# Loading one parameter tile first, moving the end of the step-size chain into round one, taking the last norm into the MLP's last round, and 128 bytes of padding in SBUF

## The chip, the cores and the metric

The kernel runs on one core of a Trainium2 chip. The metric is the device time of one execution in microseconds (us); lower is better. The kernel before took 2057.4 us in the median of three runs (2056.34 to 2058.93).

## The reference

The reference is two transformer-like blocks on 512 tokens of width 1024, all in float32. Cut to what matters here:

```python
# first block, part one: SSD mixer
u = rmsnorm(x, ssd_norm)
z, xbc, dt = split(u @ ssd_w_in)
xbc = silu(dwconv(xbc, conv_w, conv_b))          # 5 taps
dt = softplus(dt + dt_bias)                      # 512 tokens x 64
la = dt * -exp(a_log);  cum = cumsum(la) per chunk of 128 tokens, forwards and backwards
y = ssd_scan(...) both ways + x * d_skip; y = rmsnorm(y * silu(z), gnorm)
h = x + y @ ssd_w_out
# then: GLA mixer, mixing block (conv, latent attention, gates), cross attention
h = h + square(relu(rms_norm(h, norm_mlp_g) @ w_mlp1)) @ w_mlp2
return rms_norm(h, final_norm_g)                 # 512 x 1024
```

## The kernel before

**Layout and matmuls.** Activations lie transposed: `c.h`, `c.uh`, `c.ul` are eight tiles (`KT`) of 128 features by 512 tokens. A float32 product is three matmuls (`mm3`, L57 to L67): operands are split into a rounded part (`hi`, float32r) and the rest (`lo`), and lo times hi, hi times lo and hi times hi are added in PSUM. The weights come in units of 128x1024 elements. `load_unit` (SP, L112) loads one into one of `RAW` = 2 slots and waits until the unit two before it was split; `split_hi` (ScalarE, L123) rounds it into one of `WS` = 3 slots and waits for the matmuls of the unit three before; `split_lo` (VectorE, L133) makes the rest. `stream_products` (TensorE) runs a unit's 24 matmuls of 128x512 into one of `SB` = 3 PSUM banks ("stream") and waits for the bank to be free. The five other banks are `q[0]` to `q[4]`. Each engine works through its own instructions in the order of the code and waits on semaphores.

**Opening (in `ssd_stage`, first block).** SP issues the loads of x (four, L461), of two weight units, of 128 rows of `ssd_conv_w` (tile 0 of the parameter rows), of two vectors, of the other parameter rows (22 small loads for parameters in all, four tiles `c.ptiles`) and then of weight units. TensorE turns the four parameter tiles (L510), VectorE copies each to `par` (L616). ScalarE sums the squares of x (L570) and takes the rough reciprocal root (L574, L576). Only then does VectorE refine it (L170 to L176), and x is scaled by VectorE (L620) and ScalarE (L579), two row tiles each. TensorE turns the scaled x (L518), ScalarE and VectorE make `uh` (L584) and `ul` (L625) with the gain `ssd_norm`, and the product for dt (unit `first`) runs between them. Then the units `first+1` and `first+2` are streamed, and x is turned into `c.h` (L525, L599). Meanwhile VectorE works on the softplus of dt, its logarithmic decays and their sums (L631 to L661, "the step-size chain"). TensorE then turns dt, la and cum (12 small transposes, L555) once VectorE has done with `cum_l` (L666), VectorE copies them (L670 to L672), TensorE sums the columns (L559), and ScalarE and VectorE make `et`, `wc`, `lah`, `lal` (L604 to L607, L675 to L688). Last, `first+3` is streamed.

**Rounds.** A second block runs ten rounds of eight slots `(i, k)`, written out in the same order for each engine. Round 0 has the units `(0,2)`, `(0,3)`, `(0,5)`, `(0,6)`, that are `first+1` to `first+4`: x, x, B and C of group 0. The convolution of a unit stands in the slot after it: ScalarE does the middle tap (L959), VectorE the four others (L1081), which also frees the bank. At slot `(0,7)` ScalarE takes the silu (L1027, L1029), at `(1,0)` TensorE streams a unit, waits for the silu and turns the results (L913). POOL makes the decay steps (L810) from `lah`, `lal`. Blocks and stages are parted by a barrier of all engines.

**MLP and end.** `mlp_stage` streams 64 units, in turn eight that read `uh`/`ul` (first product, closed by L2747) and eight that read `ah`/`al` (second product, added to `h` at L2761). In the last eight, ScalarE squares `h` (L191) and POOL adds up the squares (L206). `norm_stage` ("last") then sums over the features with a matmul with ones (L317, or q<-h_sum_of_squares), refines the reciprocal root over 128x512 and scales all of `h` (L362). `finish_stage` turns `h` back (32 transposes, L2783), copies it to `out_rows` (L2791, L2797) and stores four row tiles (L2804).

**Where the tiles lie.** In the compiled program a tile follows the one before it in the order of the code, sizes rounded up to 32 bytes. Byte offsets in a partition, and the remainder by 256:

```
u_hi 32896 (128)         weights_hi 73856 (128)   weights_lo 86144 (128)
u_lo 49280 (128)         h_squares 102080 (192)   params 108224 (192)
ssd_y_hi 198400 (0)      merge_hi 179968 (0)      mix_cq_hi 151296 (0)
x_q_hi 184064 (0)        mlp_a_hi 118528 (0)      mlp_a_lo 134912 (0)
gla_q_hi 137152 (192)    gla_y_hi 210880 (192)
```

Parts of a tile that a matmul reads begin at multiples of 512 bytes in it, so each has the remainder of its tile.

## Time and profile before

| | |
|---|---|
| median of 3 runs | 2057.4 us (2056.34 to 2058.93) |
| the profiled execution | 2057.16 us |
| its span, first to last instruction | 2055.4 us |
| TensorE matmul busy | 1829.1 us (89%) |
| VectorE, ScalarE, GpSimd busy | 1264.9, 783.8, 418.3 us |
| mean granted TensorE clock | 0.946 |
| read from HBM, mean rate | 135.70 MB, 67 GB/s |

The span is one execution as the hardware profiler recorded it. The profiled execution took 1.8 us more than its span. PE is TensorE, PEld its weight loads, DVE VectorE, ACT ScalarE, POOL GpSimd, SPq the queue of SyncE that issues the loads. "<-" inside a name reads "written from".

### The profile page before, as it was taken

The numbers are of one execution on the slowest core, as the hardware profiler recorded it, in microseconds if no ns is written. First come the engines' busy times: TensorE is split into PE (matmuls) and PEld (weight loads), VectorE is DVE, ScalarE is ACT, GpSimd is POOL, SyncE is SP. The second block draws the span as 40 slices with busy tenths as digits, with TensorE's granted clock in tenths as the row PEclk, the third lists the DMA queues.
The fourth block names the chain that finished last, engine by engine and source line by source line (L and its number), as shares of the span: only waits on it lengthen the run. The fifth ranks groups of instructions, "written<-read, shape, count | busy, mean of one in ns | idle before, by whom it ended". The sixth has DMA issues, their size and how long they took to land. (4 is left out here: it accounts for less than half of the span.)

```text
span 2055.4 us, 21726 instructions
## 1 busy us (share of the span) xinstructions
PE 1829.1 (89%) x8186; PEld 1460.3 (71%) x8186; DVE 1264.9 (62%) x1665; ACT 783.8 (38%) x1165; POOL 418.3 (20%) x369
## 2 busy tenths in 40 slices
PE   5789999999977989999978997787899799999996
PEld 4667777777754868787856776565678778888884
DVE  4668877887766555656546779765465553434343
ACT  4432443344324352535234423344344442323232
POOL 0244644464352000000006023400021020000001
PEclk9989999999988999999988999898899999999998
DMA  3212222222101212222212322110223133333331
GB/s 92 72 42 62 62 62 62 62 62 62 62 23 53 72 41 77 68 82 62 80 44 57 92 68 65 41 25 27 92 83 102 32 91 103 93 93 102 93 93 51
DMA packets 252197, 139.19 MB, mean 68 GB/s; under 512 B 25973, under 2 KB 246558, under 8 KB 252094
## 3 DMA queue, kind: packets, MB, share of 16 engines
q1 hardware_dynamic: 252093, 137.82, 23.4%
q8 instruction: 65, 1.06, 0.2%
q14 instruction: 39, 0.31, 0.0%
HBM read 135.70 MB, written 2.10 MB: 67 GB/s over the span
## 5 line engine op out<-in xcount | busy, mean ns | idle before, releaser
L65 PE MATMUL stream<-u_lo,weights_hi 128*128 128x512 f32 (+2 forms) x1312 | 535.3, 408 | 46.8 <-DVE weights_lo L133 19.3
L133 DVE TENSOR_TENSOR weights_lo<-weights_raw,weights_hi 128x1024 fp32r<-128x1024 f32 (+4 forms) x266 | 341.0, 1282 | 308.1 <-ACT weights_hi L123 307.8
L67 PE MATMUL stream<-u_hi,weights_hi 128*128 128x512 f32 (+2 forms) x1312 | 521.1, 397 | 0.0
L66 PE MATMUL stream<-u_hi,weights_lo 128*128 128x512 f32 (+2 forms) x1312 | 521.1, 397 | 0.0
L123 ACT ACTIVATE weights_hi<-weights_raw 128x1024 fp32r<-128x1024 f32 (+4 forms) x266 | 268.1, 1010 | 470.4 <-PE stream L67 430.1
L65 PEld LDWEIGHTS stream<-u_lo,weights_hi 128*128 128x128 f32 (+2 forms) x1312 | 252.1, 192 | 123.6 <-issue 34.5
L67 PEld LDWEIGHTS stream<-u_hi,weights_hi 128*128 128x128 f32 (+2 forms) x1312 | 250.9, 191 | 56.6 <-issue 0.9
L66 PEld LDWEIGHTS stream<-u_hi,weights_lo 128*128 128x128 f32 (+2 forms) x1312 | 251.8, 192 | 54.9 <-issue 3.4
L203 POOL COPY h_sum_of_squares<-h_squares 128x512 f32<-128x512 f32 x5 | 3.2, 650 | 856.9 <-ACT h_squares L191 856.9
L67 PE MATMUL stream<-mlp_a_hi,weights_hi 128*128 128x512 f32 x256 | 101.1, 395 | 0.0
L65 PE MATMUL stream<-mlp_a_lo,weights_hi 128*128 128x512 f32 x256 | 101.1, 395 | 0.0
L66 PE MATMUL stream<-mlp_a_hi,weights_lo 128*128 128x512 f32 x256 | 101.1, 395 | 0.0
L1986 DVE SCALAR_TENSOR_TENSOR mix_conv<-mix_z,params,mix_conv 128x512 f32<-128x512 f32 x79 | 82.1, 1040 | 2.3
L769 POOL TENSOR_TENSOR ssd_y<-ssd_y,ssd_state_parts 128x384 f32<-128x384 f32 x32 | 33.1, 1035 | 190.7 <-DVE ssd_state_parts L1067 188.4
L1081 DVE SCALAR_TENSOR_TENSOR ssd_bc<-stream,params,ssd_bc 128x510 f32<-128x510 f32 (+1 forms) x64 | 48.0, 749 | 33.3 <-ACT ssd_bc L959 31.6
L206 POOL TENSOR_TENSOR h_sum_of_squares<-h_sum_of_squares,h_squares 128x512 f32<-128x512 f32 x35 | 50.7, 1447 | 73.0 <-ACT h_squares L191 71.1
L2747 DVE SCALAR_TENSOR_TENSOR mlp_relu<-stream,h_squares 128x512 f32<-128x512 f32 x32 | 22.1, 691 | 69.2 <-PE stream L67 68.9
L1961 POOL TENSOR_TENSOR mix_conv<-mix_conv,gates_tap_products 128x512 f32<-128x512 f32 x30 | 46.4, 1546 | 76.1 <-ACT gates_tap_products L1953 74.0
L65 PE MATMUL stream<-ssd_y_lo,weights_hi 128*128 128x512 f32 x128 | 53.7, 419 | 7.8 <-DVE ssd_y_lo L1169 5.2
L66 PEld LDWEIGHTS stream<-mlp_a_hi,weights_lo 128*128 128x128 f32 x256 | 48.1, 188 | 11.7
L65 PEld LDWEIGHTS stream<-mlp_a_lo,weights_hi 128*128 128x128 f32 x256 | 48.1, 188 | 11.7
L67 PEld LDWEIGHTS stream<-mlp_a_hi,weights_hi 128*128 128x128 f32 x256 | 48.0, 188 | 11.6
(494 smaller groups left out, 3368.0 us busy)
## 6 DMA issues: line engine op xcount, KB each, us to landing
weights_raw<-in_w_mlp_dram SPq DMA_DIRECT2D x64, 512.0 KB, 3.9
weights_raw<-in_ssd_w_in_dram SPq DMA_DIRECT2D x48, 512.0 KB, 3.9
weights_raw<-in_gla_w_in_dram SPq DMA_DIRECT2D x40, 512.0 KB, 3.7
weights_raw<-in_w_in_dram SPq DMA_DIRECT2D x29, 512.0 KB, 3.7
weights_raw<-in_ssd_w_out_dram SPq DMA_DIRECT2D x16, 512.0 KB, 3.5
weights_raw<-in_gla_w_out_dram SPq DMA_DIRECT2D x16, 512.0 KB, 3.3
weights_raw<-in_w_out_dram SPq DMA_DIRECT2D x8, 512.0 KB, 4.0
weights_raw<-in_w_xkv_dram SPq DMA_DIRECT2D x8, 512.0 KB, 4.2
```

Source lines behind the costliest of these rows:

```text
L65: pe.matmul(out, lh, rl, start=first, stop=False, skip_group_check=skip)
L66: pe.matmul(out, ll, rh, start=False, stop=False, skip_group_check=skip)
L67: return pe.matmul(out, lh, rh, start=False, stop=last, skip_group_check=skip)
L123: act.activation(w_view(c, n)[0], raw_view(c, n), ACT.Copy).then_inc(c.w_rounded, 1)
L133: dve.tensor_tensor(lo, raw_view(c, n), hi.bitcast(F32), ALU.subtract).then_inc(c.w_split, 1)
L203: pool.tensor_copy(acc[:, :], c.sq[:, n % 2, :]).then_inc(c.square_added, 1)
L206: pool.tensor_tensor(acc[:, :], acc[:, :], c.sq[:, n % 2, :], ALU.add).then_inc(c.square_added, 1)
L769: pool.tensor_tensor(y[:, p, a], y[:, p, a], parts[:, d * (T - P):(d + 1) * (T - P)], ALU.add).then_inc(s_fin, 1)
L1081: ins = dve.scalar_tensor_tensor(out=dst[:, a:b], in0=src[:, a + o:b + o], scalar=tap(tp, ct), in1=dst[:, a:b], op0=ALU.mult, op1=ALU.add)
L1961: pool.tensor_tensor(acc[:, LAST, :], acc[:, LAST, :], prod[:, e % 2, :], ALU.add)\
L1986: dve.scalar_tensor_tensor(out=acc[:, m, :], in0=src, scalar=par[:, w:w + 1], in1=acc[:, m, :], op0=ALU.mult, op1=ALU.add)\
L2747: dve.scalar_tensor_tensor(out=r_[:, m % 2, :], in0=bank(c, t)[:, :], scalar=0.0, in1=c.rstd, op0=ALU.max, op1=ALU.mult).then_inc(c.bank_f ...
```

## The change

1. `ssd_norm` becomes the first vector of the parameters, so tile 0 holds it and 120 rows of `ssd_conv_w`. Tile 0 is loaded before the first two weight units, the other tiles after them. VectorE waits for tile 0 only before it refines the root of x; three row tiles of x are scaled by VectorE and one by ScalarE. The other parameter tiles are turned into `q[4]` after the product for dt and copied by one VectorE instruction after the step-size chain's sums.
2. The opening's block ends with unit `first+2`. What followed `cum` (the 12 transposes, the copies, the column sums, `et`, `wc`, `lah`, `lal`) stands in slots `(0,4)` to `(0,7)`, unit `first+3` in `(0,5)`. The tiles dt, la, cum and their columns live as long as the stage (9,216 bytes a partition). ScalarE's table load at the start of the second block goes. In the opening's block units up to `first+4` are loaded and split, one fewer.
3. The last norm is made inside `mlp_stage`: `h` is scaled by the gain, turned by TensorE between the last units, and scaled by token afterwards, when the tokens lie on partitions. The stages "last" and "out" go.
4. `stage_offset`, 128 bytes a partition, is allocated ahead of `params` and all stage tiles; `gla_rstd` grows from 64 to 128 bytes. Stage tiles' offsets grow by 128, those of GLA after `rstd` by 192, all to a remainder of 128 by 256.

```diff
@@ opening, SP
+                    load_params(0)
                     for n in range(first, first + 2):
                         load_unit(c, sp, n)
+                    ... (the two vectors)
+                    for i in range(1, NP):
+                        load_params(i)
...
-                    for n in range(first + 2, first + 6):
+                    for n in range(first + 2, first + 5):
@@ opening, TensorE
                     pe.wait_ge(s_const, 1)
-                    for i in range(NP):
-                        turn_params(i)
+                    turn_params(0)
...
                     last.then_inc(c.tile_done, 1)
+                    pe.wait_ge(s_par, 1)
+                    for i in range(1, NP):
+                        turn_params(i)
...
                     stream_products(c, pe, first + 2, ...)
-                    (12 transposes, column sums, stream_products of first + 3)
@@ opening, VectorE
-                    for i in range(NP):
-                        dve.wait_ge(s_pt, i + 1)
-                        n = c.prows[i]
-                        dve.tensor_copy(c.par[:, i * P:i * P + n], c.q[i][:, 0:n]).then_inc(s_par, 1)
+                    dve.wait_ge(s_pt, 1)
+                    dve.tensor_copy(par[:, 0:P], c.q[4][:, 0:P]).then_inc(s_par, 1)
                     dve.wait_ge(s_rx, 2)
                     refine_rstd(dve, s_fine, 0, rx[:, :], tx[:, :], ssq[:, :], D)
-                    for t in (0, 1):
+                    for t in (0, 1, 2):
...
+                    dve.wait_ge(s_pt, NP)
+                    n = P * (NP - 2) + c.prows[-1]
+                    dve.tensor_copy(par[:, P:P + n], c.q[4][:, 0:n]).then_inc(s_par, 1)
@@ rounds, VectorE, after the convolution of the slot before
+                    if (i, k) == (0, 5):
+                        dve.wait_ge(s_a, 4)
+                        (cum_l)
+                        dve.wait_ge(s_t, 1)
+                        (copies dtc, lac, cumc)
+                    if (i, k) == (0, 6):
+                        dve.wait_ge(s_t, 2)
+                        (cumc = q[0] - cumc)
+                    if (i, k) == (0, 7):
+                        dve.wait_ge(s_a, 7)
+                        (wc, lah, lal)
@@ rounds, ScalarE
-                act.preload_act_table_set(LN_EXP)
...
+                    if (i, k) == (0, 5):
+                        (cum_h)
...
+                    if (i, k) == (0, 7):
+                        act.wait_ge(s_v, 18)
+                        (exp of cumc, exp of q[0], round lac)
@@ rounds, TensorE: 12 transposes at (0,4); at (0,5) after the unit:
+                        pe.wait_ge(s_v, 16)
+                        pe.matmul(q[0][:, 0:NT * 64], c.ones[:, :], flat(lac), start=True, stop=True).then_inc(s_t, 1)
@@ rounds, POOL, before the first decay steps
+                            pool.wait_ge(s_v, 21)
@@ mlp_stage, TensorE
+                def to_rows(m):
+                    pe.wait_ge(s_hg, m + 1)
+                    if m == NT:
+                        pe.wait_ge(s_half, NT)
+                    for t in range(NT):
+                        last = pe.transpose(c.q[t][:, m % NT * P:(m % NT + 1) * P], hg[:, m, t * P:(t + 1) * P],
+                                            c.ident[:, :])
+                    last.then_inc(s_tp, 1)
+                def token_sums(src, first):
+                    for t in range(NT):
+                        last = pe.matmul(c.q[4][:, t:t + 1], src[:, t * P:(t + 1) * P], c.ones[:, 0:1], ...)
...
                 for k in range(N):
+                    if k - LAST >= 2:
+                        to_rows(k - LAST - 2)
                     (unit n0 + k)
+                to_rows(KT - 2)
+                pe.wait_ge(c.square_added, squares)
+                token_sums(c.sumsq, True)
+                pe.wait_ge(c.square_ready, squares + 1)
+                token_sums(c.sq[:, squares % 2, :], False).then_inc(s_tok, 1)
+                to_rows(KT - 1)
@@ mlp_stage, ScalarE, behind the square of unit k - 1
+                    if k == LAST + 5:
+                        act.preload_act_table_set(LN_EXP)
+                        act.wait_ge(s_tp, NT)
+                        for t in range(NT):
+                            act.activation(rows[:, t, 0:T], c.q[t][:, :], ACT.Copy).then_inc(s_half, 1)
+                (rough root of q[4][:, 0:NT], 128x4: Ln, Exp)
+                act.wait_ge(s_fine, 4)
+                act.wait_ge(s_tp, KT)
+                for t in range(NT):
+                    act.activation(rows[:, t, T:D], c.q[t][:, :], ACT.Copy, scale=rt[:, t:t + 1]).then_inc(s_right, 1)
@@ mlp_stage, GpSimd
-                add_squares(c, pool)
+                add_squares(c, pool, tiles=KT - 1)
@@ mlp_stage, VectorE
+                        if k > LAST:
+                            dve.wait_ge(*free_value(c, t))
+                            dve.tensor_scalar(hg[:, m, :], c.h[:, m, :], gain(m), None, ALU.mult).then_inc(s_hg, 1)
...
+                dve.wait_ge(s_root, 2)
+                refine_rstd(dve, s_fine, 0, rt[:, :], tmp[:, :], c.q[4][:, 0:NT], D)
                 for t in range(NT):
+                    dve.wait_ge(s_half, t + 1)
+                    dve.tensor_scalar(rows[:, t, 0:T], rows[:, t, 0:T], rt[:, t:t + 1], None, ALU.mult)\
+                       .then_inc(s_left, 1)
@@ mlp_stage, SP
+                for t in range(NT):
+                    sp.wait_ge(s_left, t + 1)
+                    sp.wait_ge(s_right, t + 1)
+                    sp.dma_start(o[:, t, :], rows[:, t, :]).then_inc(c.stored, 16)
+                sp.wait_ge(c.stored, 16 * NT)
@@ build and gla_stage
+        sb("stage_offset", [P, 32])
-        ssq, rstd = sb("square_sums", [P, NT]), sb("rstd", [P, 16])[:, 0:NT]
+        ssq, rstd = sb("square_sums", [P, NT]), sb("rstd", [P, 32])[:, 0:NT]
-        norm_stage(nc, c, "last", ...)
-        finish_stage(nc, c, out)
```

## Rows read from the trace of the kernel before

**Rows 1.** The timeline, 10 to 26 us: start, length, engine, line, what, count.

```profile
10.71 0.21 ACT L576 ACTIVATE dt_x_rstd<-dt_x_rstd 128x4 f32<-128x4 f32 x1
...
17.70 0.36 SPq L476 DMA_DIRECT2D dt_skips<-in_ssd_d_dram  x1
...
19.11 0.20 DVE L616 COPY params<-q 128x41 f32<-128x41 f32 x1 [1.44 <-PE q L510]
...
20.01 2.19 ACT L579 ACTIVATE dt_x_normed<-dt_x_rows,dt_x_rstd 128x1024 f32<-128x1024 f32 x2 [9.09 <-DVE dt_x_rstd L176]
20.01 1.42 DVE L620 TENSOR_SCALAR dt_x_normed<-dt_x_rows,dt_x_rstd 128x1024 f32<-128x1024 f32 x2
...
22.25 3.67 PE L518 MATMUL q<-ident,dt_x_normed 128*128 128x128 f32 x16 [3.18 <-ACT dt_x_normed L579]
```

**Rows 2.** The timeline, 34 to 56 us, TensorE and VectorE.

```profile
34.19 1.91 PE L525 MATMUL q<-ident,dt_x_rows 128*128 128x128 f32 x16
...
51.01 1.22 DVE L661 TENSOR_TENSOR_SCAN dt_cum<-dt_restart,dt_la 32x512 f32<-32x512 f32 x1
...
54.13 0.46 PE L555 MATMUL q<-ident,dt_dt 64*128 64x64 f32 x4 [2.91 <-DVE ssd_cum_lo L666]
...
55.93 1.22 PE L559 MATMUL q<-dt_la_cols,ones 128*128 128x256 f32 x2 [0.85 <-DVE dt_la_cols L671]
```

**Rows 3.** The timeline, 55 to 84 us, by engine: TensorE, ScalarE and VectorE in round 0.

```profile
55.79 0.41 DVE L672 COPY dt_cum_cols<-q 128x256 f32<-128x256 f32 x1
...
59.68 2.35 DVE L133 TENSOR_TENSOR weights_lo<-weights_raw,weights_hi 128x1024 fp32r<-128x1024 f32 x2
...
63.77 1.28 ACT L942 ACT_TABLE_LOAD   x1 [3.23 <-PEq L457]
...
65.88 6.11 DVE L1081 SCALAR_TENSOR_TENSOR ssd_x<-stream,params,ssd_x 128x510 f32<-128x510 f32 x8 [3.85 <-ACT ssd_x L959]
...
69.13 0.76 PE L65 MATMUL stream<-u_lo,weights_hi 128*128 128x512 f32 x1 [5.64 <-DVE ssd_x L1081]
...
76.50 0.78 ACT L959 ACTIVATE ssd_bc<-stream,params 128x512 f32<-128x512 f32 x1 [6.88 <-PE stream L67]
...
77.31 3.10 DVE L1081 SCALAR_TENSOR_TENSOR ssd_bc<-stream,params,ssd_bc 128x510 f32<-128x510 f32 x4 [1.18 <-ACT ssd_bc L959]
...
83.86 1.09 PE L913 MATMUL q<-ident,ssd_x 128*128 128x128 f32 x8 [1.96 <-ACT ssd_bc L1029]
```

**Rows 4.** The timeline, 2012 to 2051 us: last units, last norm, output.

```profile
2015.28 0.63 ACT L191 ACTIVATE h_squares<-h 128x512 f32<-128x512 f32 x1 [1.89 <-DVE h L2761]
...
2017.87 0.69 DVE L2761 TENSOR_TENSOR h<-h,stream 128x512 f32<-128x512 f32 x1 [2.62 <-PE stream L67]
...
2029.07 0.69 DVE L2761 TENSOR_TENSOR h<-h,stream 128x512 f32<-128x512 f32 x1 [4.92 <-PE stream L67]
...
2050.66 0.69 DVE L2797 COPY out_rows<-q 128x512 f32<-128x512 f32 x1 [0.18 <-PE q L2783]
```

**Rows 5.** The timeline of VectorE: two closings of each kind of MLP unit.

```profile
1885.07 0.69 DVE L2747 SCALAR_TENSOR_TENSOR mlp_relu<-stream,h_squares 128x512 f32<-128x512 f32 x1 [2.41 <-PE stream L67]
...
1890.51 0.69 DVE L2747 SCALAR_TENSOR_TENSOR mlp_relu<-stream,h_squares 128x512 f32<-128x512 f32 x1 [2.41 <-PE stream L67]
...
1903.84 0.68 DVE L2761 TENSOR_TENSOR h<-h,stream 128x512 f32<-128x512 f32 x1
...
1909.43 0.68 DVE L2761 TENSOR_TENSOR h<-h,stream 128x512 f32<-128x512 f32 x1
```

**Rows 6.** The page: DMA issues, KB each, median us from issue to landing.

```profile
weights_raw<-in_ssd_w_in_dram SPq DMA_DIRECT2D x48, 512.0 KB, 3.9
```

**Rows 7.** Busy time by engine, granted clock, DMA share and rate in one stretch.

```profile
2052.00:2053.00 1.00, 0.00 (x0) 0.00 (x0) 0.00 (x0) 0.00 (x0) 0.00 (x0) 1.00 1.02 418
```

**Rows 8.** The timeline of TensorE, first and last matmul of the unbroken run over `gla_y`.

```profile
1072.66 0.41 PE L65 MATMUL stream<-gla_y_lo,weights_hi 128*128 128x512 f32 x1
...
1092.37 0.39 PE L67 MATMUL stream<-gla_y_hi,weights_hi 128*128 128x512 f32 x1
```

More of the change, by code:

```diff
@@ L191, in square_tile, with add_squares @@
         act.activation(c.sq[:, n % 2, :], c.h[:, m, :], ACT.Square).then_inc(c.square_ready, 1)
-def add_squares(c, pool, accs=None):
+def add_squares(c, pool, accs=None, tiles=KT):
     accs = accs or [c.sumsq]
-    for m in range(KT):
+    for m in range(tiles):
         for acc in accs:
@@ L462, in _, with load_params @@
                           .then_inc(s_xl[t], 16)
-                    for n in range(first, first + 2):
-                        load_unit(c, sp, n)
-                    for i, tile in enumerate(c.ptiles):
-                        for r0, view in tile:
+                    def load_params(i):
+                        for r0, view in c.ptiles[i]:
                             dst = prow[r0:r0 + view.shape[0], i, :]
@@ L550, in _ @@
                     stream_products(c, pe, first + 2, lambda j: c.uh[:, j, :], lambda j: c.ul[:, j, :])
-                    pe.wait_ge(s_v, 14)
-                    pe.wait_ge(s_h, KT)
-                    for j, src in enumerate((dt, la, cum)):
-                        for t in range(NT):
-                            last = pe.transpose(c.q[1 + j][:, t * 64:(t + 1) * 64], src[:, t * P:(t + 1) * P],
-                                                c.ident[0:64, 0:64])
-                    last.then_inc(s_t, 1)
-                    pe.wait_ge(s_v, 16)
-                    pe.matmul(c.q[0][:, 0:NT * 64], c.ones[:, :], lac[:, :, :].rearrange("p t h -> p (t h)"),
-                              start=True, stop=True).then_inc(s_t, 1)
-                    stream_products(c, pe, first + 3, lambda j: c.uh[:, j, :], lambda j: c.ul[:, j, :])
                 @block.scalar
@@ L1038, in _ @@
             def _(dve):
-                for n in range(first, first + 2):
-                    split_lo(c, dve, n)
                 taps = [0]
@@ L2674, in cross_stage, with mlp_stage @@
         cross_out_stage(nc, c, A, qh, ql, gain)
-def mlp_stage(nc, c, A):
+def mlp_stage(nc, c, A, out, gain):
     CH = FF // D
@@ L2691, in mlp_stage @@
         tile = lambda k: c.tiles_before[n0 + k]
+        hg = sb("h_scaled", [P, KT, T])
+        rows = sb("out_rows", [P, NT, D])
+        rt, tmp = sb("token_rstd", [P, NT]), sb("token_newton", [P, NT])
+        o = out[0].rearrange("(t p) d -> p t d", p=P)
+        s_hg, s_tp, s_half, s_tok, s_root, s_fine, s_left, s_right = (sem(n) for n in (
+            "h_scaled", "transposed", "first_half", "token_sums", "token_rstd_s", "token_refined",
+            "left_rows", "right_rows"))
+        squares = c.added + KT - 1
+        LAST = N - KT
         with nc.Block() as block:
```

149 lines of the change are left out of this document (60 added, 89 removed).

## The prediction

> **What bounds the kernel now.** First the page: TensorE is busy for 89% of the span, and in the MLP its 64 units follow each other without a gap. So there are two ways to a shorter time: fewer stretches in which TensorE stands, and a closer sequence of matmuls where it doesn't. I then read the timeline at both ends. At the start the first transposes of x begin at 22.25 us, because the last parameter copy on VectorE began only at 19.11 and the refined root stands behind it; the rough root was there at 10.92 [rows 1]. In round 0 TensorE stands twice more: 2.91 us for the step-size chain, and 5.64 us for a bank that the taps free [rows 2, 3]. At the end, TensorE does its last streamed matmul just before 2029.07, and 26.3 us follow in which the norm and the output run one after the other [rows 4]. Last, I compared the closings of MLP units: one that reads `u` takes 5.44 us, one that reads `mlp_a` 5.59, with the same weights, shapes and engines [rows 5].
>
> All sums are in the profiled execution's time: span 2055.4, and 2057.16 with what lies around it (1.8 us), which is within 0.3 us of the median of 2057.4.
>
> **Part 1, the opening.** The rough root stands at 10.92. Parameter tile 0 is now issued right behind x, and x was in before the root was taken, so I take it as landed and copied by 10.9, when the root needs it. From the start of the last copy to the start of the scaling took 0.90 us before (19.11 to 20.01), so scaling starts at 11.8. VectorE scaled two row tiles in 1.42, so three take 2.13: 13.95. ScalarE does its one tile (1.10) and the rounding inside that. TensorE starts at about 14.0 instead of 22.25: **8.3 us earlier** [rows 1]. What could be late next: the queue of SP. It has the same loads in another order and ends them at about 18.1 as before [rows 1]; only then does it issue unit `first+2`. A unit lands 3.9 us after its issue [rows 6], so at 22; it is due after the transposes of x that began at 34.19 and unit `first+1`, so after 41 minus 8.3. That leaves 10 us of cover [rows 2]. The 22 small loads are no longer in anyone's way: their transposes (three, under 0.5 us) stand after the dt product, and it is VectorE's chain, for which TensorE waits 2.91 us later, that sets the end of this block [rows 2]. Bounds: 6 us if tile 0 lands 2 us after the root, 8.5 if all goes at once.
>
> **Part 2, the chain into round 0.** I keep the old times here; all are 8.3 lower in fact. The scans end at 52.23 [rows 2]. Then VectorE copies the other parameters (0.47, from 0.41 for 256 columns), does the three small copies (0.5) and splits two units (2.35) [rows 3]: 55.6. The barrier took 0.28 before (the last matmul ended 5.64 before 69.13, at 63.49; the first instruction behind it is at 63.77), so round 0 starts at 55.9 instead of 63.77. The table load (1.28) is gone from it: the first taps start 0.8 after the start, at 56.7, and their 8 take 6.11: 62.8. Now the moved work: `cum_l` and three copies, each started before the one ahead has ended, 1.75 (0.41 is the row for a copy, 0.7 for twice its width), 64.6, and the split of `first+5` 1.2, 65.8. TensorE meanwhile does 12 transposes (0.95) and unit `first+3`. It starts after 5 us of rest, so at the lower level of its clock (1.2 GHz), as the unit at 69.13 did, with 7.3 us for 24 matmuls: 64.3. Its middle tap (0.78) is done when VectorE comes. Taps 3.1: 68.9. The column sums (0.66) go ahead of `first+4` on TensorE, 65.0; that unit 5.5, 70.5; middle tap, 71.3; taps, 74.4. Before, these taps ended at 80.41 [rows 3]. So another **6.0 us**. `wc`, `lah`, `lal` (1.1 us on VectorE, then POOL's four steps) are late next: POOL can start at 75.6 and needs 4.2, and the first decay sums come some 8 us after the transposes at 77.9. ScalarE's three small ones (1.2) stand before the silu but are done at 72.5. Queued behind TensorE's wait for `lac` is only `first+4`; `lac` is copied at 64.2, before the unit ends. Bounds: 4 (the taps of B wait, each moved copy counts fully) to 7.
>
> **Part 3, the end.** Added inside the loop: six groups of four transposes. Sixteen took 1.91, so 0.12 each and 2.9 us, on a TensorE that never waits there. `to_rows(4)` waits for `s_half`: the square of the unit ended at 2015.91, then comes the table load 1.28 and four copies of about 0.5 (squares of that size take 0.63), so 2019.2; TensorE gets there 0.5 after 2017.8, at 2018.3 [rows 2, 4]. So 0.9 more. Scaling by the gain on VectorE (8 of under 0.7) is hidden: between two closings 5.6 us apart VectorE has one split (1.2) and the addition (0.68) to do [rows 5].
> After the last closing (2029.07, call it T): `h` 0.69, square 0.63, so T+1.4; the first half of the token sums and `to_rows(6)` run under that. The second half is eight passes of one column. No row shows one: below by the 0.12 of a transpose, above by the 0.6 of a pass over 256 columns [rows 2]; nearest is the transpose, a load of 128 columns and little else, so 1.0. T+2.4. Ln and Exp on 128x4 0.8 with their starts, refinement 0.8, four scaled copies 2.0 (VectorE's four lie beside them). The first row tile can go at T+4.7, the last at T+6.1. The store moves 2.1 MB; in the stretch where it is alone it went at 418 GB/s [rows 7], so 5.0 us in all, 1.25 a tile. Before, the end came 4.05 after the last row tile was copied (2051.35 to 2055.4) [rows 4]. So not before T+6.1+4.05, T+10.2, and at most three tiles' transfers behind the first tile's 4.05, T+12.5. Four issued within 1.4 us are bound by the transfer, so near the upper end: T+11.9. Before, it was T+26.3. **14.4 less 3.8 is 10.6 us.** Bounds: 8 (token sums at the upper bound, copies one by one) to 12.5.
>
> **Part 4, the padding.** Offsets of `u` and of the weights leave 128 by 256. `mlp_a`, `merge`, `x_q`, `mix_cq` and `ssd_y` leave 0, GLA's leave 192. Two MLP units differ by 0.16 us over 24 matmuls, so 226.7 against 233 ns from start to start [rows 5]. The unbroken run over `gla_y`, 86 steps, gives 19.71/86 = 229.2 [rows 8], in between, at a third remainder. That the level goes with the remainder and not with the stage is shown by the MLP, where both kinds alternate. If a remainder of 128 gives 226.7 to all: MLP 32 units, 5.1 us; 384 `ssd_y`, 192 `merge`, 96 `x_q`, 120 latent matmuls at 0.0067 are 5.3, of which I count 3.3, since TensorE partly waits for VectorE in those stages; 384 `gla_y` at 0.0025 1.0. Sum **9.4 us**. What stays open is whether 256 is the period: by 512 the moved tiles leave 384, `u` 128. Bounds: none at all to 12. I take the full value, as five families of tiles fit it.
> The Trainium skill ("TensorE: Matmul & The Clock Gate", section "Wait — 56ns, not 53.3ns?") gives a warm matmul of 512 columns 215.7 ns from start to start, whatever its operands' addresses; by it this part would be worth nothing. The trace doesn't agree: it has 226.7 and 233.
>
> **Sum.** 8.3 + 6.0 + 10.6 + 9.4 = 34.3. 2055.4 - 34.3 = 2021.1, and with 1.8 around the span **2022.9 us**.
>
> **Rivals.** (a) The remainder isn't the cause, and the padding does nothing. For it: every slower family also lies above 110,000 bytes, `u` below 66,000; against it: `gla_y` lies highest of all and is the middle one. 2032.3. Chance 0.13. "SBUF — State Buffer", section "Who interferes with whom", of the Trainium skill would side with it: PE never waits on anyone. (b) The transposes break the stream of the last round: the wait for `s_half` or another one lets the clock fall, and nine matmuls run at 0.43 instead of 0.23, as after 69.13 [rows 3], and each of the six groups costs 0.3 more when TensorE changes between kinds. +1.8 and +1.8: 2026.5. For it, the clock did fall after 5.6 us of standing; against, this wait is 1 us. Chance 0.08. (c) The loads are late: unit `first` and `first+1` now stand behind tile 0, and ScalarE's rounding of a unit that has not landed holds up all that stands behind it, `uh` too. If the dt product then starts 8.3 us later than said, where it did before, 2031.2. Against it, two small loads are all that goes ahead of them. Chance 0.04. (d) Slower: the new remainder by 512 is a worse one. Some 1900 matmuls move, and the other parts give 24.9 us, so this decides from 13 ns more for each, twice the difference between the levels seen. The price at three times that difference, 20 ns, is 38 us: 2070. Chance 0.02. That the change does nothing in parts 1 and 3 I can exclude: 26 us of serial work are taken out.
>
> **How the numbers follow.** The forecast has 0.73, with an own range of 2019 to 2027. To hold 8 in 10 with (b) and most of (a), the range is 2018.5 to 2032.8. 0.2% (4.1 us) is about what a measurement of this kernel can tell from no change. Faster 0.97; same 0.01; slower 0.02.
>
> **What would show it.** The transposes of scaled x start at 14.0; those after the silu 14.3 earlier than 83.86, at 69.6. MLP units over `mlp_a` close every 5.44 us instead of 5.59; if it is 5.59, (a) holds. In the last round one gap of 0.9 us ahead of the fifth group of transposes. From the last closing to the end of the span 12 us. The forecast is wrong above all if the remainder does nothing, or if the moved tiles fall on a third level.

## The result and the profile after

The changed kernel takes 2024.44 us in the median of four runs (2023.38 to 2032.84); the kernel before, run beside it, 2058.16 (2056.34 to 2064.12). The ratio is 0.9841, with a 95% interval of 0.9818 to 0.9863. The profiled execution took 2024.04, its span is 2022.3. The forecast was 2022.9 (2018.5 to 2032.8) and "faster" at 0.97.

The page of the changed kernel: the span, and TensorE's busy time.

```profile
span 2022.3 us, 21708 instructions
...
PE 1813.3 (90%) x8200; PEld 1456.5 (72%) x8200; DVE 1259.3 (62%) x1664; ACT 782.1 (39%) x1167; POOL 414.5 (20%) x368
```

TensorE does almost the same matmuls and is busy 15.8 us less than the 1829.1 of before. Of that, 3.4 lie ahead of the transposes after the silu and 4.8 behind the last matmul over `mlp_a`; the other 7.6 lie between, where the same work runs closer together. The rest of the 33.1 us of span is standing time: 21.5 us less at the two ends, some 4 us more between them.

**The opening.** The timeline of the changed kernel, all engines, from the rough root to the first transposes (start, length, engine, line, what, count, what it waited for).

```profile
10.26 0.44 PE L510 MATMUL q<-ident,dt_param_rows 128*128 128x128 f32 x1 [10.26 <-DMA dt_param_rows<-in_ssd_conv_w_dram]
...
10.74 0.29 DVE L595 COPY params<-q 128x128 f32<-128x128 f32 x1 [10.74 <-PE q L510]
...
11.16 0.21 ACT L565 ACTIVATE dt_x_rstd<-dt_x_rstd 128x4 f32<-128x4 f32 x1
...
12.20 2.08 DVE L599 TENSOR_SCALAR dt_x_normed<-dt_x_rows,dt_x_rstd 128x1024 f32<-128x1024 f32 x3
...
14.33 3.29 PE L516 MATMUL q<-ident,dt_x_normed 128*128 128x128 f32 x16 [3.63 <-DVE dt_x_normed L599]
```

The one parameter copy is over when the rough root comes at 11.37 (11.16 and 0.21), so nothing stands ahead of the refinement any more. The transposes start at 14.33 instead of 22.25 [rows 1]: 7.9 earlier.

**Round 0.** The timeline of VectorE, ScalarE and TensorE from the last parameter copy to the transposes after the silu.

```profile
42.82 0.47 DVE L644 COPY params<-q 128x297 f32<-128x297 f32 x1
...
46.52 1.45 ACT L937 ACTIVATE ssd_x<-stream,params 128x512 f32<-128x512 f32 x2 [5.61 <-PEq L454]
...
47.34 6.11 DVE L1062 SCALAR_TENSOR_TENSOR ssd_x<-stream,params,ssd_x 128x510 f32<-128x510 f32 x8 [1.10 <-ACT ssd_x L937]
...
56.09 3.09 DVE L1062 SCALAR_TENSOR_TENSOR ssd_bc<-stream,params,ssd_bc 128x510 f32<-128x510 f32 x4
...
62.00 3.10 DVE L1062 SCALAR_TENSOR_TENSOR ssd_bc<-stream,params,ssd_bc 128x510 f32<-128x510 f32 x4 [1.36 <-ACT ssd_bc L937]
...
68.56 1.09 PE L892 MATMUL q<-ident,ssd_x 128*128 128x128 f32 x8 [1.97 <-ACT ssd_bc L1012]
```

From the end of the scans (42.8) to the round's first instruction it is 3.7 us, where the forecast had 52.23 to 55.9. The last taps end at 65.1, 18.6 after the round's start, where the forecast had 74.4 - 55.9 = 18.5. The transposes start at 68.56 instead of 83.86 [rows 3], 15.3 earlier (forecast 14.3).

**The last round.** VectorE's closings of two pairs of units over `mlp_a` and over `u`, then ScalarE, VectorE and TensorE at the fifth group of transposes.

```profile
1904.87 0.68 DVE L2814 TENSOR_TENSOR h<-h,stream 128x512 f32<-128x512 f32 x1
1910.31 0.68 DVE L2814 TENSOR_TENSOR h<-h,stream 128x512 f32<-128x512 f32 x1
...
1929.78 0.69 DVE L2800 SCALAR_TENSOR_TENSOR mlp_relu<-stream,h_squares 128x512 f32<-128x512 f32 x1 [2.41 <-PE stream L67]
1935.22 0.69 DVE L2800 SCALAR_TENSOR_TENSOR mlp_relu<-stream,h_squares 128x512 f32<-128x512 f32 x1 [2.41 <-PE stream L67]
...
1994.09 0.63 ACT L191 ACTIVATE h_squares<-h 128x512 f32<-128x512 f32 x1 [1.89 <-DVE h L2814]
...
1994.74 1.28 ACT L2770 ACT_TABLE_LOAD   x1
...
1996.03 2.06 ACT L2773 ACTIVATE mlp_out_rows<-q 128x512 f32<-128x512 f32 x4
...
1997.73 0.49 DVE L2818 TENSOR_SCALAR mlp_h_scaled<-h,params 128x512 f32<-128x512 f32 x1
...
1998.24 0.63 PE L2720 MATMUL q<-ident,mlp_h_scaled 128*128 128x128 f32 x4 [1.27 <-DVE mlp_h_scaled L2818]
```

A unit over `mlp_a` now closes after 5.44 us, as one over `u` does; before it was 5.59 [rows 5]. The only gap in the round is the 1.27 us ahead of the fifth group. The profile puts it down to `mlp_h_scaled`. But the fifth group needs the fifth of those tiles, and it was there at 1994.6; what ended last before TensorE went on were ScalarE's four copies, at 1998.09.

**The end.** The timeline from the last closing, then the stretch in which the store is alone (length, busy time of five engines, granted clock, DMA share, GB/s).

```profile
2010.29 0.69 DVE L2814 TENSOR_TENSOR h<-h,stream 128x512 f32<-128x512 f32 x1 [4.71 <-PE stream L67]
...
2011.69 1.05 PE L2726 MATMUL q<-ones,h_squares 128*128 128x1 f32 x8 [0.22 <-ACT h_squares L191]
...
2012.79 0.26 ACT L2775 ACTIVATE mlp_token_rstd<-q,eps 128x4 f32<-128x4 f32 x1 [1.14 <-PE q L2726]
...
2014.11 2.42 ACT L2782 ACTIVATE mlp_out_rows<-q,mlp_token_rstd 128x512 f32<-128x512 f32 x4 [0.82 <-DVE mlp_token_rstd L176]
...
2014.87 2.92 SPq L2710 DMA_DIRECT2D out_dram<-mlp_out_rows  x4
```
```profile
2018.00:2019.00 1.00, 0.00 (x0) 0.00 (x0) 0.00 (x0) 0.00 (x0) 0.00 (x0) 0.50 1.04 414
```

With T = 2010.29: root begun at T+2.5 (forecast 2.4), first store at T+4.6 (4.7), last copy over at T+6.2 (6.1), end at T+12.0 (11.9). Before, the end came 26.3 after the last closing [rows 4].

### The profile page after: what moved, and what is told of

Read it like the earlier page. It is cut to its first block and busy times, and to the rows that moved or that the text cites. A ratio compares the mean times of both kernels' runs of the same rounds, so it can differ in the third digit from the quotient of the medians.

```text
span 2022.3 us, 21708 instructions
## 1 busy us (share of the span) xinstructions
PE 1813.3 (90%) x8200; PEld 1456.5 (72%) x8200; DVE 1259.3 (62%) x1664; ACT 782.1 (39%) x1167; POOL 414.5 (20%) x368
## 5 line engine op out<-in xcount | busy, mean ns | idle before, releaser
L734 POOL TENSOR_TENSOR ssd_y<-ssd_y,ssd_state_parts 128x384 f32<-128x384 f32 x32 | 33.1, 1034 | 191.9 <-DVE ssd_state_parts L1048 189.6
L819 PE MATMUL q<-ssd_m,ssd_x_pair 128*128 128x128 f32 x256 | 36.5, 287 | 22.4 <-DVE ssd_m L1145 22.4
L65 PE MATMUL stream<-gla_y_lo,weights_hi 128*128 128x512 f32 x128 | 50.9, 398 | 5.8 <-DVE gla_y_lo L1597 5.8
```

What stands on the lines that cost most here:

```text
L65: pe.matmul(out, lh, rl, start=first, stop=False, skip_group_check=skip)
L734: pool.tensor_tensor(y[:, p, a], y[:, p, a], parts[:, d * (T - P):(d + 1) * (T - P)], ALU.add).then_inc(s_fin, 1)
L819: last = pe.matmul(q[p][:, t * P:(t + 1) * P], xp[:, t, p, a], mm[:, t % 2, 2 * p + h, :], start=h == 0, stop=h == 1, skip_group_check=True)
```

## The experiments

The whole time can't carry all of these readings. The same stretch of the same code differs by some microseconds from one traced execution to another, as the middle columns show. So each experiment is read first in the stretch that its edit touches. Durations in us, from the starts of named instructions in each kernel's trace:

| kernel | first transpose of scaled x | to first transpose of x | to transposes after silu | to last `ssd_y` matmul | to last `gla_y` matmul | to first `mlp_a` matmul | first to last `mlp_a` | to end of span | span |
|---|---|---|---|---|---|---|---|---|---|
| before | 22.25 | 11.94 | 49.67 | 555.83 | 452.68 | 626.73 | 309.54 | 26.76 | 2055.4 |
| e2_padding_alone | 23.12 | 11.11 | 51.55 | 554.59 | 450.75 | 625.11 | 304.41 | 26.96 | 2047.6 |
| changed | 14.33 | 10.92 | 43.31 | 554.50 | 450.90 | 627.14 | 308.76 | 12.44 | 2022.3 |
| e1_no_padding | 14.41 | 12.05 | 43.92 | 557.43 | 455.12 | 624.21 | 313.51 | 12.25 | 2032.9 |
| e9_old_end | 14.36 | 11.45 | 43.58 | 557.02 | 454.81 | 622.25 | 304.41 | 28.32 | 2036.2 |
| e10_units_first | 16.16 | 12.14 | 43.95 | 557.19 | 452.42 | 625.02 | 308.80 | 12.42 | 2028.1 |
| e11_chain_back | 13.67 | 11.06 | 50.04 | 557.00 | 454.80 | 624.40 | 308.81 | 12.42 | 2032.2 |
| e8_copies_first | 14.67 | 12.44 | 44.11 | 557.47 | 454.92 | 618.49 | 307.33 | 12.46 | 2021.9 |
| e12_x_first_and_copies_first | 14.27 | 11.36 | 43.54 | 553.54 | 449.12 | 620.46 | 307.33 | 12.48 | 2012.1 |

### The padding taken away, and the padding alone

```diff
@@ e1_no_padding: the changed kernel
-        sb("stage_offset", [P, 32])
-        ssq, rstd = sb("square_sums", [P, NT]), sb("rstd", [P, 32])[:, 0:NT]
+        ssq, rstd = sb("square_sums", [P, NT]), sb("rstd", [P, 16])[:, 0:NT]
@@ e2_padding_alone: the kernel before
+        sb("stage_offset", [P, 32])
-        ssq, rstd = sb("square_sums", [P, NT]), sb("rstd", [P, 16])[:, 0:NT]
+        ssq, rstd = sb("square_sums", [P, NT]), sb("rstd", [P, 32])[:, 0:NT]
```

> The changed kernel without the padding (stage_offset away, gla_rstd back to 64 bytes). Theory (the start of a moving operand modulo 256 bytes sets the pace of a matmul): MLP units over mlp_a close every 5.60 us again, the time is 7.6 us above the changed kernel's (the sum of the leads that the two traces show outside the opening and the end), about 2032. Rival (the padding does nothing, the closer pace came with the other edits): the units keep 5.45 us and the time stays at 2024.

> The kernel before with the padding alone. Theory: 7 to 9 us less than before, 2049 to 2051, MLP units over mlp_a at 5.45 us. Rival: 2057.5 and 5.60 us.

Measured: without padding 2031.44 us (2026.98 to 2038.46), ratio to before 0.9863 (0.9828 to 0.9898). Padding alone 2050.32 (2046.19 to 2051.28), ratio 0.9945 (0.9927 to 0.9963). Before was at 2061.59 beside both. Two units over `mlp_a` without padding:

```profile
1897.48 0.68 DVE L2814 TENSOR_TENSOR h<-h,stream 128x512 f32<-128x512 f32 x1
1903.08 0.68 DVE L2814 TENSOR_TENSOR h<-h,stream 128x512 f32<-128x512 f32 x1
```

They are back at 5.60 us. By the table the padding alone takes 309.54 - 304.41 = 5.1 us from the MLP and 7.8 from the span. The units show in both directions that it does something, and rival (a) is out. Of the whole time e2 shows it clear of noise: 11.3 us between the medians, more than the 7 to 9 that I expected. e1 alone doesn't: it is 7.0 above the changed kernel in the median, but 4.5 by the two ratios to the kernel before, whose intervals overlap.

### Which remainder counts: that of the moving operand, or its distance from the weights

```diff
@@ e3_padding_384: the changed kernel, 256 bytes more
-        sb("stage_offset", [P, 32])
+        sb("stage_offset", [P, 96])
@@ e4_everything_128_on: the changed kernel; u, weights and stage tiles all 128 bytes on
+        sb("all_offset", [P, 32])
         c.h = sb("h", [P, KT, T])
@@ e5_weights_128_on: the changed kernel; only the split weights 128 bytes on
+        sb("weights_offset", [P, 32])
         c.w_hi, c.w_lo = sb("weights_hi", [P, WS, UNIT], F32R), sb("weights_lo", [P, WS, UNIT], F32R)
+        sb("weights_offset_back", [P, 32])
@@ e6_padding_64 (and e7_padding_192 with 48 instead of 16)
-        ah, al = sb("a_hi", [P, KT, T], F32R), sb("a_lo", [P, KT, T], F32R)
+        ah = sb("a_hi", [P, KT, T], F32R)
+        sb("a_offset", [P, 8])
+        al = sb("a_lo", [P, KT, T], F32R)
-        sb("stage_offset", [P, 32])
+        sb("stage_offset", [P, 16])
```

> The changed kernel with 384 bytes of stage_offset in place of 128: the remainder by 256 stays 128, that by 512 goes from 384 to 128. Period 256 or a divisor of it: same time as the changed kernel (2024) and 5.45 us a unit. Period 512: another pace, up to 5.60 us a unit and some 8 us more, or a closer pace than 5.45.

> The changed kernel with 128 bytes ahead of all tiles, so that the moving operands (u and the stages' tiles) and the weights all lie at remainder 0. If the moving operand's own remainder counts: every streamed matmul takes 233 ns, that of u too (some 5800 of them at 6.6 ns more, less what hides under other waits): 30 to 38 us above the changed kernel, 2054 to 2062. If the distance between moving operand and weights counts: it is unchanged at 0, so the time is 2024.

> The changed kernel with only the split weights moved by 128 bytes (remainder 0 by 256), all moving operands left at 128. Theory (what counts is the distance between the moving operand and the weights, modulo 256; 0 is fast, 128 is slow): every streamed matmul of 512 columns goes from 0.227 to 0.233 us from start to start, u and mlp_a alike; MLP units close every 5.60 us instead of 5.44 in both kinds. Some 3600 steps over u and 1900 over the others at 0.0064 are 35 us, of which 25 to 35 show in the time: 2049 to 2059. Rival (only the moving operand's own start counts): no change, 2024.4, and 0.227 everywhere.

> The changed kernel with 64 bytes of padding instead of 128, and 32 bytes between mlp_a_hi and mlp_a_lo: stage tiles at a remainder of 64, mlp_a_lo at 96, the weights at 128. Distance theory: at a distance of 64 the pace is the middle one that gla_y had at 192, 0.229; so gla_y, merge, ssd_y go to about 0.229, mlp_a to 0.229 or a little less (a third of its matmuls have a distance of 32), and the time is 3 to 4 us above that of the changed kernel. Rival (only one remainder, 128, is good and all others cost alike): 0.233 and some 7 us.

> The same with 192 bytes of padding: stage tiles at a remainder of 192, mlp_a_lo at 224, distances 64 and 96 on the other side. Distance theory, symmetric: the same 0.229 as with 64 for gla_y, merge and ssd_y; mlp_a_lo, at a distance of 96, nearer to 0.231. 3 to 5 us above the changed kernel. Rival (the order of the two addresses counts): 64 and 192 give different levels, one of them 0.227.

Measured: e3 2026.17 us (2015.42 to 2028.98), ratio 0.9825 (0.9788 to 0.9862); e4 2026.31 (2023.79 to 2030.51), ratio 0.9839 (0.9805 to 0.9872); e5 2046.46 (2042.54 to 2047.38), ratio 0.9945 (0.9926 to 0.9964); e6 2031.33 and e7 2032.59, one run each. So e5 is 22.0 above the changed kernel, where I expected 25 to 35, and e6 and e7 are 6.9 and 8.2 above it, where I expected 3 to 4 and 3 to 5. The first and last matmul of the unbroken runs over `gla_y`, of 85 steps in e5, then 82 in e6, then 82 in e7, in three fences:

```profile
1070.66 0.39 PE L66 MATMUL stream<-gla_y_hi,weights_lo 128*128 128x512 f32 x1
...
1090.40 0.39 PE L67 MATMUL stream<-gla_y_hi,weights_hi 128*128 128x512 f32 x1
```
```profile
1064.36 0.39 PE L66 MATMUL stream<-gla_y_hi,weights_lo 128*128 128x512 f32 x1
...
1083.49 0.40 PE L67 MATMUL stream<-gla_y_hi,weights_hi 128*128 128x512 f32 x1
```
```profile
1066.30 0.39 PE L66 MATMUL stream<-gla_y_hi,weights_lo 128*128 128x512 f32 x1
...
1085.07 0.39 PE L67 MATMUL stream<-gla_y_hi,weights_hi 128*128 128x512 f32 x1
```

That is 19.74/85 = 232.2, 19.13/82 = 233.3 and 18.77/82 = 228.9 ns from start to start. And two closings each of the two kinds of MLP unit in e5:

```profile
1902.47 0.68 DVE L2814 TENSOR_TENSOR h<-h,stream 128x512 f32<-128x512 f32 x1
1908.06 0.68 DVE L2814 TENSOR_TENSOR h<-h,stream 128x512 f32<-128x512 f32 x1
...
1961.53 0.69 DVE L2800 SCALAR_TENSOR_TENSOR mlp_relu<-stream,h_squares 128x512 f32<-128x512 f32 x1 [2.54 <-PE stream L67]
1967.11 0.69 DVE L2800 SCALAR_TENSOR_TENSOR mlp_relu<-stream,h_squares 128x512 f32<-128x512 f32 x1 [2.54 <-PE stream L67]
```

In e5 no moving operand was touched, and the units over `u` went from 5.44 to 5.58 us with the others. In e4 all remainders are 0 and the units over `mlp_a` stay at 5.44:

```profile
1890.61 0.68 DVE L2814 TENSOR_TENSOR h<-h,stream 128x512 f32<-128x512 f32 x1
1896.05 0.68 DVE L2814 TENSOR_TENSOR h<-h,stream 128x512 f32<-128x512 f32 x1
```

So it is not the moving operand's own remainder but its distance from the weights, modulo 256. Where the `hi` and the `lo` part of the moving operand lie at the same distance, the traces give:

| moving operand less weights, modulo 256 | ns from start to start | seen in |
|---|---|---|
| 0 | 227 | changed, e3, e4: `mlp_a`, `gla_y`; `u` in all but e5 |
| 64 | 229 | before and e7: `gla_y`; e7: `x_q` (but `merge` 231) |
| 128 | 232 to 233 | before and e1: `mlp_a`, `merge`, `x_q`; e5: all |
| 192 | 233 | e6: `gla_y`, `merge` |

These are means. Over `mlp_a` in the kernel before, half of the steps take 229 or 230 ns and half 237 or 238. Other engines aren't the cause: the 302 steps during which neither ScalarE nor VectorE nor GpSimd runs an instruction have a mean of 233.7 ns, the 462 others 233.1.

My expectation for e6 was wrong. The levels aren't symmetric: 64 bytes ahead of the weights is the middle level, 64 bytes behind them the worst. That the period is 256 and not 512 follows from e3: the distance from the weights was 256 modulo 512 in the changed kernel and is 0 there, and both give 5.44.

Two readings show that the table isn't the whole rule. In e6 and e7 `mlp_a_hi` and `mlp_a_lo` lie at different distances (192 and 224, and 64 and 96), and units over `mlp_a` close every 5.55 us in both, 231.1 ns a matmul. There the steps differ by place: in e6 236.6 ns after a matmul over the `lo` part, 227.7 and 229.3 after the two over the `hi` part, for which the table has 233. So the pace also goes by which matmuls follow each other.

The products of `gla_v` with `gla_k` in `q` don't read the split weights at all, and their two operands have the same remainder in every kernel, distance 0. Still their 45 steps (longer ones than 245 ns left out) have means of 229.0 ns before, 226.9 in the changed kernel and 227.2 in e4, but 230.7 in e5, where only the split weights changed their remainder, and 230.8 in e6 and 229.1 in e7. That is the order of the table if `gla_v` is compared with the split weights instead of with `gla_k`. The products of `gla_v` with `gla_att` follow it less (228.6 in e5, 226.7 in e6). What in the chip makes these levels is open.

The Trainium skill ("SBUF — State Buffer", section "Who interferes with whom") gives TensorE two read ports, one for the moving operand and one for the weights, independent of each other. e5 is hard to square with that: moving the weights alone slowed matmuls whose moving operand stayed where it was. No run here shows which part of the chip is shared.

### The old end

e9_old_end is the changed kernel with `mlp_stage`, `norm_stage` ("last") and `finish_stage` of the kernel before.

```diff
-        mlp_stage(nc, c, A, out, col("final_norm_g_2"))
+        mlp_stage(nc, c, A)
+        norm_stage(nc, c, "last", hk, KT, col("final_norm_g_2"), None, None, plain=hk, summed=True)
+        finish_stage(nc, c, out)
```

> The changed kernel with the end of the kernel before: the MLP's last round without the scaling and the transposes, then the stages for the last norm and the output. Theory: from the last closing to the end of the span 26.3 us instead of 12.0, and the last closing 4.1 us earlier (six groups of transposes at 0.47 and the wait of 1.27 are gone): 10.2 us slower, 2034.6. Rival (the transposes in the loop lay in time that TensorE had anyway, so the whole 14.3 is gained): 2038.7, with the last closing at the same time.

Measured: 2037.57 us (2035.46 to 2041.82), ratio 0.9909 (0.9885 to 0.9932). In the MLP it is 308.76 - 304.41 = 4.35 us shorter, so the rival (transposes in time that TensorE had anyway) is out. The tail is 28.32 instead of 12.44, 15.9 more, where 14.3 were expected; the two traces with the same old end show 26.76 and 26.96. The difference lies behind the last copy, which is over at 2030.9, 5.3 before the end; in the kernel before that was 4.05. So the new end is worth 14.3 to 15.9 less 4.35, 10.0 to 11.5. The rest of the 13 us between the medians can't be given to the edit: in columns that it doesn't touch, `ssd_y` and `gla_y` took 6.4 longer than in the changed kernel's trace, and the stretch to the first `mlp_a` matmul 4.9 less.

### The order of the loads in the opening

```diff
@@ e10_units_first
-                    load_params(0)
                     for n in range(first, first + 2):
                         load_unit(c, sp, n)
+                    load_params(0)
```

> The changed kernel with its opening waits, but with the loads in the old order: the first two weight units are issued ahead of parameter tile 0. Theory: the larger part of the opening's gain is that the root waits for one tile and not for four, the smaller one that this tile is loaded early. Seven loads in, SP's queue stood for 4.5 us in both kernels (4.32 to 8.94 and 5.00 to 9.46); tile 0 falls behind that again, and its second piece is issued at 9.3 and landed at about 12.5. Copied at 13.0, root refined at 13.9, scaled at 16.0: the transposes of scaled x at 16.1 instead of 14.33, and 1.8 us on the time, 2026.2. Rival (the order of the loads does all of it): transposes at 22 and 2032. Second rival (the order does nothing): 14.3 and 2024.4.

Measured: 2030.21 us (2026.7 to 2030.87), ratio 0.9855 (0.983 to 0.9881). The timeline of SP's queue and TensorE in e10:

```profile
4.45 4.65 SPq L465 DMA_DIRECT2D dt_param_rows<-in_ssd_norm_dram  x1
9.14 0.34 SPq L465 DMA_DIRECT2D dt_param_rows<-in_ssd_conv_w_dram  x1
...
12.55 0.45 PE L510 MATMUL q<-ident,dt_param_rows 128*128 128x128 f32 x1 [12.55 <-DMA dt_param_rows<-in_ssd_conv_w_dram]
```

The tile came at 12.55 and the transposes started at 16.16 (expected 16.1), 1.8 later than in the changed kernel. So of 7.9 us the order of loads gives 1.8, and waiting for one tile instead of four 6.1. The median is 4 us higher than expected. The trace shows 2.7 more in `ssd_y` and 1.5 more in `gla_y`, and 2.1 less in the stretch behind, all untouched by the edit.

### The chain back in the opening

```diff
@@ e11_chain_back, TensorE, behind unit first+2 (ScalarE's and VectorE's parts as before)
+                    (12 transposes, column sums)
+                    stream_products(c, pe, first + 3, lambda j: c.uh[:, j, :], lambda j: c.ul[:, j, :])
@@ rounds
-                    if (i, k) == (0, 4): (12 transposes)
-                    if (i, k) == (0, 5): (column sums)
```

> The changed kernel with the end of the step-size chain back in the opening's block (12 transposes, copies, column sums, et, wc, lah, lal, then unit first+3), but without the table load at the start of the rounds. Theory: of the 5.9 us of this part the table load ahead of the first taps was 1.3, so 4.6 remain: the transposes after the silu at 73.2 instead of 68.56, and 2029.0. Rival (the table load was hidden, the chain is all of it): 74.5 and 2030.3. Second rival (round 0 waits for the taps in any case, so moving the chain gains only the stall of 2.9): 71.5 and 2027.3.

Measured: 2034.24 us (2025.41 to 2036.1), ratio 0.987 (0.984 to 0.99). From the first transposes of x to those after the silu it is 50.04, against 43.31 to 44.11 in the six traces above with the chain in the round: 5.9 to 6.7. I expected 4.6, since ScalarE's table load (1.28) at the start of the rounds is not in e11. That was wrong. The first rival's number, 5.9, came out, but not its reason, that the table load was hidden: from the first transposes of x to VectorE's first taps e11 takes 31.1 us, the kernel before 31.7. TensorE, which stands for 4.4 us until the taps free a bank, shows why:

```profile
59.12 0.77 PE L65 MATMUL stream<-u_lo,weights_hi 128*128 128x512 f32 x1 [4.36 <-DVE ssd_x L1082]
...
63.95 0.63 PE L67 MATMUL stream<-u_hi,weights_hi 128*128 128x512 f32 x1
...
65.15 0.39 PE L65 MATMUL stream<-u_lo,weights_hi 128*128 128x512 f32 x1
```

Twelve matmuls run at 0.43 us from start to start, so at the lower level of the clock, before the pace of 0.23 returns. In the kernel before it was eight there and four in the unit behind the chain; in e11 it is twelve and seven. Seven matmuls more at 0.43 instead of 0.23 are 1.4 us: the longer stretches of low clock in this execution took back what the missing table load gave.

### The copies ahead of the square, and x ahead of the weights

```diff
@@ e8_copies_first, ScalarE in the last round
+                    if k == LAST + 5:
+                        (table load, wait, four copies)
                     if k > LAST:
                         square_tile(c, act, k - 1 - LAST, free_value(c, tile(k - 1)))
-                    if k == LAST + 5:
-                        (table load, wait, four copies)
@@ e12_x_first_and_copies_first: also, SP in the opening
                     load_params(0)
+                    sp.wait_ge(s_xl[2], 16)
                     for n in range(first, first + 2):
```

> The changed kernel with ScalarE's table load and its four copies of the first half of the rows put ahead of the square of the same step instead of behind it. Theory (the wait of 1.27 ahead of the fifth group of transposes is for these copies and not for h scaled by the gain, which the profile names): the copies are done some 2 us before TensorE comes, the wait is gone, and the time is 1.3 lower, 2023.1. Rival (TensorE waits for h scaled by the gain): the gap stays at 1.27, 2024.4.

> The same as e8, and SP waits until the third row tile of x has landed before it issues the first two weight units. Theory: x shares its transfer with 0.75 MB of weights (its four row tiles landed 1.4, 2.6 and 1.6 us apart, where 512 KB at 418 GB/s are 1.25), so the last one lands some 1.2 us earlier, and all behind it moves by as much: transposes of scaled x at 13.1, time 2021.9. Rival (the first unit, issued at 6.6 instead of 3.45, lands too late for ScalarE at 12 and holds up uh behind it): the dt product starts no earlier than 17.38, and 2023.1 or more.

Measured: e8 2027.43 us (2023.63 to 2031.24), ratio 0.9848 (0.9822 to 0.9874); e12 2020.2 (2013.78 to 2024.23), ratio 0.9808 (0.9782 to 0.9833). The timeline of e8 at the fifth group of transposes:

```profile
1994.52 2.06 ACT L2771 ACTIVATE mlp_out_rows<-q 128x512 f32<-128x512 f32 x4
...
1997.59 0.39 PE L67 MATMUL stream<-mlp_a_hi,weights_hi 128*128 128x512 f32 x1
1997.82 0.60 PE L2720 MATMUL q<-ident,mlp_h_scaled 128*128 128x128 f32 x4
```

The gap is gone: the transposes follow the last matmul of the unit after 0.23. The MLP takes 307.33 instead of 308.76 us in both e8 and e12, 1.4 less (expected 1.3). So TensorE did wait for the copies and not for what the profile named. The median doesn't show it: it is 3.0 above the changed kernel's, not 1.3 below.

In e12 the four squares of x, each of which starts when its row tile has landed, start so:

```profile
4.12 1.06 ACT L560 ACTIVATE dt_squares<-dt_x_rows 128x1024 f32<-128x1024 f32 x1 [2.04 <-DMA dt_x_rows<-in_x_dram]
...
5.56 1.06 ACT L560 ACTIVATE dt_squares<-dt_x_rows 128x1024 f32<-128x1024 f32 x1 [0.29 <-DMA dt_x_rows<-in_x_dram]
...
8.19 1.06 ACT L560 ACTIVATE dt_squares<-dt_x_rows 128x1024 f32<-128x1024 f32 x1 [1.48 <-DMA dt_x_rows<-in_x_dram]
```

The units were issued at 8.18 instead of 3.45, and yet the third tile came at 8.19 (8.00 in the changed kernel) and the fourth at 9.53 (9.60). My theory that the weights take bandwidth from x has fallen; what holds up the third tile is open. The transposes of scaled x start at 14.27, inside the 13.46 to 14.67 of the eleven traces with the new order of loads.

So e12 has the lowest median of all kernels run, but only 1.4 us of that are explained by its edits. Against e8 it is 7.2 lower in the median and 9.8 in the span. Of the 9.8, 3.9 lie in the column of `ssd_y` and 5.8 in that of `gla_y`, in code that is the same in both. Whether the later issue of two loads brings this about or it fell so is not settled. One execution of e3, which has neither edit, took 2015.42, near e12's fastest of 2013.78, and both show a mean granted clock of 0.955, the highest of all.

## Why the prediction was right, step by step

**Part 1, the opening: 8.3 forecast, right.** The two traces with the old opening have the transposes of scaled x at 22.25 and 23.12, the eleven with the new one at 14.31 in the mean: 8.4. e10 shows how it divides. All three things that could have been late next were not: SP's unit `first+2` was issued at 17.59 and landed in time, the transposes of the other parameters took 0.56 behind the dt product, and the chain still set the block's end. In the profile the lead at the end of the scans is 9.4. The excess over 7.9 lies around the dt product: the stretch up to the first transposes of x takes 10.92 against 11.94, although it now holds the three transposes of the other parameters (0.5). I can't give it to the change: in the other traces with the new opening that stretch takes 11.06 to 12.44, and with the old one 11.11 and 11.94.

**Part 2, the chain: 6.0 forecast, right.** 15.3 less the 9.4 of the opening is 5.9, and e11 gives 5.9 to 6.7. The steps inside hold too (3.7 against 3.67 to the start of the round, 18.6 against 18.5 to the end of its last taps). What the sum had not foreseen is that the stretches of low clock are not the same from one execution to the next, which is worth as much as the table load in it.

**Part 3, the end: 14.4 less 3.8 forecast, 14.3 less 4.35 measured.** The tail came out step by step, within 0.1 us each. The price inside the loop was 0.5 too low: six groups take 0.47 each in the stream, 2.8 (2.9 forecast), but the wait for `s_half` is 1.27 and not 0.9, and some 0.3 more lies around the groups. For the wait, the copies were over 3.37 after the square (3.3 forecast) and TensorE was there 2.26 after it (2.4 forecast): both a little off, in the same direction. Net 10.0, forecast 10.6.

**Part 4, the padding: 9.4 forecast, 7.8 in the pair of e2 and the kernel before.** The MLP's 5.1 is right to the decimal, since TensorE never waits there. How much of the other 4.3 came isn't settled. By the span it is 2.7 (7.8 less 5.1). But that includes 1.9 us that e2 lost between the transposes of x and those after the silu, where the streamed matmuls read `u`, which the padding doesn't move; in the three columns with moved tiles ahead of the MLP e2 is 4.8 shorter. In each of these columns traces with the same code and offsets differ by about as much as the whole term, or more. So I can't say whether taking 3.3 of 5.3 for `ssd_y`, `merge`, `x_q` and the latent matmuls was too much. That the level follows the remainder by 256 was right for this layout; as a rule it was incomplete, as it is the distance from the weights. Rival (d), a worse level at the new offsets, did not come: the padding makes that distance 0, the level of `u`.

**The Trainium skill's figure.** "TensorE: Matmul & The Clock Gate", section "Wait — 56ns, not 53.3ns?", has 215.7 ns for a warm matmul of 512 columns, without a word on the addresses of its operands. No stream in any trace here came to it: the best distance gives 227, the worst 233.

**The sum.** 15.3 (parts 1 and 2) and 10.0 (part 3) leave 7.8 of the 33.1 of the span, against 34.3 forecast. The 7.8 are a remainder and hold whatever the untouched stretches did. That the forecast came within 1.5 us of the median is partly luck: the column of `gla_y` alone ranges from 449.1 to 454.9 in kernels that have the same code and offsets there. Rivals (b) and (c) did not come: the clock did not fall at the gap of 1.27 (the next matmuls run at 0.23), and unit `first` was split at 13.25, as soon as x was scaled.

## What to carry to other kernels

Where matmuls stream without a gap, measure the pace from start to start for each moving operand. If it has levels, look at the distance in SBUF between that operand and the weights modulo 256 bytes, and try padding to 0, with both parts of a split operand at the same distance; here 128 bytes were worth 5.1 us in the MLP and 7.8 in the span of e2. Where several small loads and copies stand ahead of one that matters, what counts is which of them the next step really waits for: that gave 6.1 of 7.9 us, and the order of the loads 1.8. Read an edit worth less than a few microseconds in its own stretch of the trace, not in the median.

## What the runs showed of the hardware that I had not expected

**Pace of TensorE.** In an unbroken stream a matmul of 128x512 in float32r repeats on average after 227, 229 or 233 ns according to the distance between its moving operand and the split weights modulo 256 (0; 64; 128 or 192), as far as both parts of the moving operand lie at the same distance. At 64 one stream, `merge` in e7, had 231.

**The same code, different stretches.** From the silu transposes of round 0 to the last matmul over `ssd_y` the traces of the table take 553.5 to 554.6 or 557.0 to 557.5 us (before 555.83). The granted clock of 75 to 200 us is one place in which they differ: it is 0.96 in the changed kernel, e2 and e12, which have 553.5 to 554.6, and 0.91 or 0.92 in the others. e12 first, then e8 (columns as in the windows above).

```profile
75.00:200.00 125.00, 112.63 (x521) 89.98 (x520) 96.82 (x121) 45.15 (x60) 59.02 (x50) 0.96 0.21 59
```
```profile
75.00:200.00 125.00, 114.02 (x507) 91.53 (x506) 96.08 (x118) 43.23 (x61) 56.42 (x48) 0.92 0.21 58
```

**SP's queue.** Behind four tiles of x and two weight units the next load, a small one, isn't issued at once: it stood for 4.62 us in the kernel before, 4.46 in the changed one and 4.65 in e10. In e12, where the units are issued at 8.18, it takes 0.79. A load that is urgent belongs ahead of this point.
